# Rows of the experts added by TensorE as products with diagonal weight matrices in the closing stage of a hybrid-trunk kernel

## What is computed

```python
h_res = h_res + concat([y_conv, y_attn, y_hgrn]) @ w_out[l]
h_res = h_res + _hier_moe(_rmsnorm(h_res, ffn_norm[l]), ...)   # y = sum over 2 experts of weight * row
return _rmsnorm(h_res, final_norm)[:, N_META:]

def _rmsnorm(x, g):
    y = xf * lax.rsqrt(jnp.mean(xf * xf, axis=-1, keepdims=True) + EPS)
    return y * g
```

## Time and profile before

| | |
|---|---|
| time, median of 3 runs | 526.74 us (524.3 to 526.88) |
| time of the profiled execution | 522.46 us |
| its span, first to last instruction | 520.6 us |
| mean granted TensorE clock in it | 0.97 |
| PE busy | 482.1 us (93%) |
| DVE busy | 284.5 us (55%) |
| ACT busy | 154.7 us (30%) |
| DMA, mean over the span | 275 GB/s |

### The profile page before, as it was taken

The page is one execution under the profiler, slowest core; times in us unless marked ns, Lnnn a source line. Parts: engine busy times, 40 slices in busy tenths (PEclk is TensorE's granted clock), DMA queues, the critical chain, the costliest instruction groups (busy, mean ns, idle before and its releaser), DMA issues.

```text
span 520.6 us, 11031 instructions
## 1 busy us (share of the span) xinstructions
PE 482.1 (93%) x4503; PEld 323.9 (62%) x4503; DVE 284.5 (55%) x694; ACT 154.7 (30%) x386; POOL 48.6 (9%) x58
## 2 busy tenths in 40 slices
PE   5999999999998899999999999999999999895772
PEld 4888889888786455456556556575565555354430
DVE  3787998899668856337364433333343222231267
ACT  6420267410345334221134322222122111111143
POOL 3410000000001000000111011312102111000000
PEclk9999999999999999999989999999999999977887
DMA  8990000000009899419887999999999999999984
GB/s 277 356 374 36 0 2 0 1 1 1 3 7 358 287 421 412 186 42 364 278 299 299 353 403 346 409 414 418 416 415 412 418 415 416 416 417 416 413 330 162
DMA packets 38020, 143.03 MB, mean 275 GB/s; under 512 B 5166, under 2 KB 12519, under 8 KB 29393
## 3 DMA queue, kind: packets, MB, share of 16 engines
q1 hardware_dynamic: 31920, 131.03, 64.4%
q0 software_dynamic: 5760, 10.89, 5.9%
q10 hardware_dynamic: 288, 0.39, 0.2%
HBM read 133.73 MB, written 17.30 MB: 290 GB/s over the span
## 4 chain that ended last, share of the span: by engine, by line
PE 73%; DMA 11%; DVE 9%; SPq 3%; issue 2%; ACT 1%; POOL 1%; DVEq 0%; POOLq 0%
PE bank L1534 12%; PE bank L1872 11%; PE bank L1736 11%; PE bank L1880 6%; PE bank L1895 6%; DMA area_g<-in_w_exp_up 5%; PE bank L1544 4%; DMA area_g<-expert_out 4%; PE bank L1903 3%; PE bank L1474 3%; PE bank L1865 3%; PE bank L1678 2%; DVE area_m L932 2%; SPq L513 1%; DMA expert_out<-area_m,cst 1%
## 5 line engine op out<-in xcount | busy, mean ns | idle before, releaser
L1736 PE MATMUL bank<-area_w,area_m 128*128 128x512 f32 x128 | 56.7, 594 | 0.4 <-issue 0.4
L932 DVE SCALAR_TENSOR_TENSOR area_m<-area_g,cols,area_m 128x512 f32<-128x512 f32 x60 | 41.4, 745 | 0.0
L1872 PE MATMUL bank<-area_w,area_m 128*64 128x256 f32 x320 | 39.9, 394 | 1.2 <-ACT area_m L1984 1.2
L1736 PEld LDWEIGHTS bank<-area_w,area_m 128*128 128x128 f32 x128 | 23.6, 190 | 26.9 <-issue 26.9
L1872 PEld LDWEIGHTS bank<-area_w,area_m 128*64 128x64 f32 x320 | 22.7, 141 | 16.5 <-issue 5.1
L1872 PE MATMUL bank<-area_g,area_m 128*64 128x256 f32 x256 | 31.1, 384 | 0.7 <-DMA area_g<-in_w_exp_up 0.7
L2097 DVE COPY cst<-bank 128x128 f32<-128x128 f32 (+1 forms) x38 | 9.9, 261 | 32.1 <-PE bank L1886 23.4
L2106 DVE TENSOR_TENSOR cst<-cst,bank 64x128 f32<-64x128 f32 x20 | 5.9, 293 | 38.4 <-ACT cst L2022 33.3
L2115 DVE COPY area_m<-bank 64x512 f32<-64x512 f32 x20 | 13.9, 694 | 22.8 <-PE bank L1895 22.7
L1880 PE MATMUL bank<-area_w,area_m 128*32 128x128 f32 x576 | 22.4, 307 | 3.7 <-DMA area_w<-in_w_exp_up 3.7
L1872 PEld LDWEIGHTS bank<-area_g,area_m 128*64 128x64 f32 x256 | 17.3, 136 | 12.4 <-issue 3.9
(11 more groups left out here) (443 smaller groups left out, 898.0 us busy)
## 6 DMA issues: line engine op xcount, KB each, us to landing
area_w<-in_w_exp_gate SPq DMA_DIRECT2D x14, 1024.0 KB
area_w<-in_w_exp_up SPq DMA_DIRECT2D x14, 1024.0 KB
area_g<-in_w_exp_gate SPq DMA_DIRECT2D x14, 1024.0 KB, 17.2
area_g<-in_w_exp_up SPq DMA_DIRECT2D x14, 1024.0 KB, 18.2
area_g<-in_w_exp_down SPq DMA_DIRECT2D x14, 1024.0 KB
area_w<-in_w_exp_down SPq DMA_DIRECT2D x14, 1024.0 KB, 16.5
area_w<-in_w_in SPq DMA_DIRECT2D x7, 1024.0 KB, 14.4
area_w<-in_w_out SPq DMA_DIRECT2D x2, 2048.0 KB, 17.2
```

The costliest lines, as they stand in the source:

```text
L932: ins = V.scalar_tensor_tensor(out=mixT[:, i, :], in0=src, scalar=w, in1=mixT[:, i, :], op0=ALU.mult, op1=ALU.add)
L1736: ins = T.matmul(bank[7][:, :], mixT[:, k, j * P:(j + 1) * P], w_out_sb[:, n, k, :], start=(k == 0), stop=(k == KT - 1))
L1872: ins = T.matmul(out_b[h * BC:(h + 1) * BC, 0:2 * P], x[:, k, :], w_gate_up[slot][:, :, k, h * P:(h + 1) * P], start=(k == 0), stop=(k == ...
```

## The change

The banks of PSUM are declared in pairs, so that one instruction of DVE or ACT can read 1024 columns (two banks). Each tile's whole sum is to stand in one pair (`total[j]`). For tiles 1 to 3 PE adds everything: the residual as a product with the identity, the last column as before, and the two expert rows of each token as products with two diagonal 128 x 128 matrices that hold the tile's weights (`rows_weighted`). DVE makes these six matrices (`row_weights`) between `gated(40)` and `act_turned(40)`, in the space that slot 6's weights have left. ACT's statistics and DVE's norm then read the sums from the banks. Tile 0 is added by DVE as before. The residual product of tile 1 takes tile 2's place before block 41's gate and up products, and that of tile 2 goes between block 41's down product and the wait for its copied rows.

```diff
-        bank = [ctx.enter_context(nc.psum_tensor(f"bank{i}", [P, 512], F32)) for i in range(8)]
+        bank_pair = [ctx.enter_context(nc.psum_tensor(f"bank_pair{i}", [P, 1024], F32)) for i in range(4)]
+        bank = [bank_pair[i // 2][:, i % 2 * 512:(i % 2 + 1) * 512] for i in range(8)]
...
-        MIX_BANK = ((2, 3), (1, 4), (7, 0), (5, 6))
-        WHOLE = 2
+        SUM_PAIR = (2, 1, 0, 3)
+        total = [bank_pair[i][:, :] for i in SUM_PAIR]
+        weight_of = [area_x[:, 0:2 * ET * P].rearrange("p (j k n) -> p j k n", j=ET, k=2)[:, j] for j in range(ET)]
+        ROOM_FROM = max(LAST_OF[RING - 1::RING]) + 1
...
-            for j in range(NT):
-                act.wait_ge(summed, j + 1)
-                row_stats(j, 0)
+            act.wait_ge(summed, 1)
+            row_stats(0, 0, xr[0])
+            for j in range(1, NT):
+                act.wait_ge(mixed, j + 1)
+                row_stats(j, 0, total[j])
...
+            def row_weights():
+
+                dve.wait_ge(gu_done, ROOM_FROM)
+                for j in range(1, NT):
+                    for k in range(2):
+                        V.tensor_scalar(weight_of[j - 1][:, k, :], ident, w_rest[:, k, j:j + 1], None, ALU.mult).then_inc(diag_ready, 1)
...
                 y_out(b_ - 1)
                 gated(b_)
+                if b_ == NB - 2:
+                    row_weights()
...
-                dve.wait_ge(mixed, 2 * j + 2)
-                for n in range(2):
-                    h = slice(n * 512, (n + 1) * 512)
-                    ins = V.tensor_tensor(xr[j][:, h], bank[MIX_BANK[j][n]][:, :], xr[j][:, h], ALU.add)
-                ins.then_inc(summed, 1)
-
-            def token_sums(j):
-
-                dve.wait_ge(d_x[j], 16 + 32)
-                for n in range(2):
-                    dve.wait_ge(mixed, 2 * j + n + 1)
-                    h = slice(n * 512, (n + 1) * 512)
-                    V.scalar_tensor_tensor(out=xr[j][:, h], in0=ye[0][:, j, h], scalar=w_rest[:, 0, j:j + 1],
-                                           in1=bank[MIX_BANK[j][n]][:, :], op0=ALU.mult, op1=ALU.add).then_inc(first_sum, 1)
-                dve.wait_ge(first_sum, 2 * j + 2)
-                V.scalar_tensor_tensor(out=xr[j], in0=ye[1][:, j, :], scalar=w_rest[:, 1, j:j + 1], in1=xr[j],
-                                       op0=ALU.mult, op1=ALU.add).then_inc(summed, 1)
+                dve.wait_ge(mixed, j + 1)
+                V.tensor_tensor(xr[j], total[j], xr[j], ALU.add).then_inc(summed, 1)
...
-            for j in range(WHOLE):
-                rows_ahead(j)
-            for j in range(WHOLE):
-                last_added(j)
-            row_norm(0, 0)
-            for j in range(WHOLE, NT):
-                token_sums(j)
-                row_norm(j - 1, 0)
-            row_norm(NT - 1, 0)
+            rows_ahead(0)
+            last_added(0)
+            row_norm(0, 0, xr[0])
+            for j in range(1, NT):
+                row_norm(j, 0, total[j])
...
+            def rows_weighted(j, last):
+
+                pe.wait_ge(d_x[j], 16 + 32)
+                for k in range(2):
+                    for o, h in halves_of(j):
+                        ins = T.matmul(o, weight_of[j - 1][:, k, :], ye[k][:, j, h], start=False, stop=last and k == 1)
+                return ins
...
             def last_rows():
 
+                resid_in(2, True)
                 pe.wait_ge(y_lo, NB)
                 pe.wait_ge(y_hi, NB)
-                for j in range(NT):
-                    if j == ET:
-                        resid_in(j)
-                    for n in range(2):
-                        T.matmul(bank[MIX_BANK[j][n]][:, :], mix_flat[0:LAST_ROWS, j * P:(j + 1) * P],
-                                 yb[LAST % 2][0:LAST_ROWS, n * 512:(n + 1) * 512], start=j < WHOLE, stop=True).then_inc(mixed, 1)
+                last_column(0, True, True).then_inc(mixed, 1)
+                pe.wait_ge(diag_ready, 2 * ET)
+                for j in range(1, ET):
+                    rows_weighted(j, False)
+                    last_column(j, False, True).then_inc(mixed, 1)
+                last_column(ET, True, False)
+                resid_in(ET, False)
+                rows_weighted(ET, True).then_inc(mixed, 1)
...
                     pe.wait_ge(mix_ready, 3)
-                    for j in range(WHOLE, ET):
-                        resid_in(j)
+                    resid_in(1, True)
```

More of the change, by code:

```diff
@@ L2074, in experts_scalar @@
                     act.wait_ge(m_xT, m + 1)
-                    A_.activation(xT_half(0, 0), bank_half(0), ACT.Copy).then_inc(m_xTa, 1)
+                    A_.activation(xT_half(0, 0), bank_half(0), ACT.Copy).then_inc(m_xTr, 1)
                     act.wait_ge(m_gu, m + 1)
@@ L2192, in row_norm @@
                 for c in [slice(0, D)] if j < NT - 1 else [slice(0, D // 2), slice(D // 2, D)]:
-                    V.scalar_tensor_tensor(out=ye[0][:, j, c], in0=xr[j][:, c], scalar=rstd[:, j:j + 1], in1=gain_out[:, c],
+                    V.scalar_tensor_tensor(out=ye[0][:, j, c], in0=src[:, c], scalar=rstd[:, j:j + 1], in1=gain_out[:, c],
                                            op0=ALU.mult, op1=ALU.mult).then_inc(o_ready, 1)
-            for j in range(WHOLE):
-                rows_ahead(j)
-            for j in range(WHOLE):
-                last_added(j)
-            row_norm(0, 0)
-            for j in range(WHOLE, NT):
-                token_sums(j)
-                row_norm(j - 1, 0)
-            row_norm(NT - 1, 0)
+            rows_ahead(0)
[3 more added lines that the diff above has]
+                row_norm(j, 0, total[j])
             with dve.If(more > 0):
+                for j in range(1, NT):
+                    V.tensor_copy(xr[j], total[j]).then_inc(summed, 1)
                 with dve.Fori(0, more) as m:
                     dve.wait_ge(m_xT, m + 1)
-                    V.tensor_copy(xT_half(0, 1), bank_half(1)).then_inc(m_xTv, 1)
+                    V.tensor_copy(xT_half(0, 1), bank_half(1)).then_inc(m_xTr, 1)
                     dve.wait_ge(m_sg, m + 1)
@@ L2219, in experts_vector @@
                 for j in range(NT):
-                    row_norm(j, NT)
+                    row_norm(j, NT, xr[j])
         def experts_tensor(pe):
@@ L2289, in gain_spread, with halves_of, resid_in, last_column @@
                          start=True, stop=True).then_inc(mix_turned, 1)
-            def resid_in(j):
+            def halves_of(j):
+                return [(total[j][:, h], h) for h in (slice(0, 512), slice(512, D))]
+            def resid_in(j, first):
                 if j == ET:
                     pe.wait_ge(d_spill, 32)
-                for n in range(2):
-                    T.matmul(bank[MIX_BANK[j][n]][:, :], ident, xr[j][:, n * 512:(n + 1) * 512], start=True, stop=False)
+                for o, h in halves_of(j):
+                    T.matmul(o, ident, xr[j][:, h], start=first, stop=False)
+            def rows_weighted(j, last):
+                pe.wait_ge(d_x[j], 16 + 32)
+                for k in range(2):
+                    for o, h in halves_of(j):
+                        ins = T.matmul(o, weight_of[j - 1][:, k, :], ye[k][:, j, h], start=False, stop=last and k == 1)
+                return ins
+            def last_column(j, first, last):
+                for o, h in halves_of(j):
+                    ins = T.matmul(o, mix_flat[0:LAST_ROWS, j * P:(j + 1) * P], yb[LAST % 2][0:LAST_ROWS, h], start=first, stop=last)
+                return ins
             def last_rows():
+                resid_in(2, True)
                 pe.wait_ge(y_lo, NB)
                 pe.wait_ge(y_hi, NB)
-                for j in range(NT):
-                    if j == ET:
-                        resid_in(j)
-                    for n in range(2):
-                        T.matmul(bank[MIX_BANK[j][n]][:, :], mix_flat[0:LAST_ROWS, j * P:(j + 1) * P],
-                                 yb[LAST % 2][0:LAST_ROWS, n * 512:(n + 1) * 512], start=j < WHOLE, stop=True).then_inc(mixed, 1)
+                last_column(0, True, True).then_inc(mixed, 1)
[6 more added lines that the diff above has]
+                rows_weighted(ET, True).then_inc(mixed, 1)
             def x_of(k):
```

19 lines of the change are left out of this document (9 added, 10 removed).

## The result

The changed kernel took 529.66 us in the median of 20 runs (527.69 to 534.23), the kernel before 526.0 us (521.11 to 529.2, 20 runs on the same chips). The ratio is 1.0108, with a 95% interval of 1.0085 to 1.0132: 1.1% slower, some 5.7 us (4.5 to 6.9). The medians differ by less, 3.7 us: the runs of the kernel before fall into a group up to 524.4 us and one from 525.8 us on, and their median lies at the edge between the two, while the means differ by 5.4 us. One run of a later version (528.52 us, the work shared, run once more) was in the slower of the chip's two states and isn't in that version's ratio. The profiled execution of the changed kernel took 529.36 us, with a span of 527.5 us, 6.9 us more than that of the profile before.

The account below looks back on a forecast made before the run. DVE's 19 us of additions and norms were taken to set the end. PE's end at 520.49 plus 0.07, 1.75 and 3.96 gave a 526.27 us span, +5.7 on 526.74: 532.4 us, range 529.0 to 535.0.

Parts of the forecast that it names:

- The tail's share: From the last column's first product to the end of the span: forecast 501.41 to 526.27, against 20.55 us before.
- The head's: From block 40's first product to the last column's first: 1.36 us later, all from the six matrices.
- The price of a product and their count: From the last column on: PE has 22 products instead of 10, at 0.86 us each, with 0.16 us behind the last.
- Behind PE's end: Tile 3's statistics and norm: 0.07 us to ACT's start, 1.75 to the norm, 3.96 to the span's end; bank reading 0.
- The six matrices: On DVE between gated(40) and block 40's copy: six at 0.286 us, copy 1.36 us late, none of it regained.
- Tile 2's residual hidden at no cost, full clock behind it: Behind block 41's down product: two products, 1.72 us, fit the 1.76 us wait for ACT's copies; 0 at full clock.
- Rival 1: Half clock again for 3.4 us around 500 us, tile 2's residual no longer hidden: +7.4 us, 534.1 us; chance 0.19.
- Rival 2: Closing stage: tile 0's reloaded rows land later than profiled, moving the kernel before more: +3.7 us, 530.4 us; chance 0.13.
- Rival 3: Closing stage: a diagonal product costs PE under 0.60 us; at 0.43 us the change is -3.8 us, 522.9 us; chance 0.04.
- Rival 4: Change not felt: matrices hidden, rows late, clock full throughout; +2.3 us, 529.0 us, within no change; chance 0.09.

Follow-up runs that it names:

- the work shared, run once more: Repeat against the kernel before: DVE adds expert rows of tiles 1 and 2, PE all of tile 3, matrices behind gated(41); ratio 0.9933.
- tile 3 alone: Against the kernel before: only tile 3 added wholly by PE, its matrices behind gated(41), no residual products between blocks 40 and 41; ratio 0.999.
- The shared version: Against the kernel before: DVE adds expert rows of tiles 1 and 2, PE their residuals and all of tile 3; ratios 0.9972 and 0.9933.

## Why the prediction was right

The forecast was 526.74 us plus 5.7 us; the ratio gives 5.7 us. The mechanism is the forecast one: PE's products become the end of the kernel. The tail's share was forecast as 4.31 us (526.27 - 501.41 less 20.55) and came as 4.33. The head's was forecast as 1.36 us, and its parts came otherwise, one smaller and one that the sum didn't have; that the whole is met to a tenth of a us is luck, as the ratio is only known to 1.2 us either way. In absolute time the median of 529.66 us is 2.7 us under the forecast of 532.4 and only 0.7 us above the lower end of the range, since 526.74 was the median of three runs and the medians differ by less than the ratio says.

- **The price of a product and their count**: 22 x 0.86 + 0.16 = 19.08 us was forecast from the last column's first product to PE's end; it was 19.12 (502.62 to 521.74). Leaving out six took 5.18 us off the tail. This is the main term, and it is shown.
- **Behind PE's end**: 0.07, 1.75 and 3.96 us were forecast; 0.03 (521.74 to 521.77), 1.71 (to 523.48) and 4.0 (to 527.5) came. Reading the bank pair costs nothing:

```profile
L2192 DVE SCALAR_TENSOR_TENSOR area_w<-bank_pair,stat,gain_out 128x1024 f32<-128x1024 f32 x2 | 2.6, 1282 | 6.3 <-ACT stat L2069 6.3
...
L2192 DVE SCALAR_TENSOR_TENSOR area_w<-w_sums,stat,gain_out 128x1024 f32<-128x1024 f32 x1 | 1.3, 1285 | 1.8 <-ACT stat L2069 1.8
```

  These groups of the changed kernel have the norm at 1282 ns out of the banks and 1285 ns out of SBUF.
- **The six matrices**: 1.36 us of delay were forecast, 0.97 us came. The term was mis-sized: each is 280 ns long, which is what I had taken, but six in a row end after 1.26 us, since one starts 0.2 us behind the other. I had multiplied a duration where the distance of starts counts. That an fp32 `tensor_scalar` in SBUF runs at twice the one-element rate, as the Trainium skill (VectorE: DVE Perf Modes, the perf-mode tier table) states, can't be read from six instructions of one size.
- **Tile 2's residual hidden at no cost, full clock behind it**: right. The control without it cost 3.5 us in the tail.
- **What the sum didn't have**: half the clock between block 40 and block 41. Rival 1 had its mechanism, but behind 500 us; there the clock was full in every version with the gap filled, and the half clock was ahead of it instead. In the two profiles of the changed kernel it is worth 1.4 us (0.87 on the down product and 0.57 on the residual) and 1.7 us (3.67 less 1.98 on the residual). The +6.9 us between the two first spans are 0.97 + 1.44 + 4.33 and 0.1 us that came before. How much of the 1.4 us the average run has isn't shown: moving the matrices took 1.9 us off, give or take 2.2, and 0.97 of that would be the delay alone.
- **Rival 2** (rows late): PE never waited for a row in any profile. The 4.28 us between the profiled execution and the median, which the prediction could not place, are of the size of what the second profile of the kernel before had, 3.6 us, and there they came from the half clock in the mixer. Rows and PE moved together by 3.7 us, as the prediction's argument against this rival had it. **Rival 3** (a product under 0.60 us): it is 0.86. **Rival 4** (+2.3 us) is out by the interval, which begins at 4.5 us, and so is rival 1 as a whole (+7.4 us): the interval ends at 6.9.

What stays open is what puts the half clock into the head. In three profiles (changed, matrices behind gated(41), shared once more) it goes on from block 40 without a break. There the wait for the matrices can't be its cause: in the changed kernel the clock was at half ahead of the wait, and the other two have no such wait. Among the profiles whose clock was full at block 40's transpose, it fell in two of the three with that wait (not with one expert row left out), and in none of the five without it that have tile 1's residual products there. That leans to a second effect of the wait, and is no proof. Why the half clock sometimes outlasts block 40 no run here shows.

## What to carry to other kernels

Before work is handed to an idle engine, price it in that engine's own rows and compare with the slack that it has: here PE had 6 us and was given 12 products, 10.3 us, at 0.86 us for what costs DVE 0.65 to 0.7 us. Share such a stage until both engines end together, and put what one engine owes another (here the matrices) where the receiver is waiting for something else anyway. An idle stretch of PE isn't free to make. Filling one of 1.8 us won 3.5 us; taking two products (1.72 us) out of a stretch that ends with a transfer saved nothing and cost 1.5 to 3.2 us of clock behind it.

## What the runs showed that I had not expected

- DVE instructions that don't need each other's result overlap by some 0.08 us: six matrices of 280 ns end after 1.26 us, four after 0.88, two after 0.48, while a row addition that reads the sum of the one before it starts 0.03 us behind that one's end.
- The stretch between block 40 and block 41 can't be shortened by removing products: block 41's weights land 7.5 us behind block 40's (488.24 to 495.77 with the matrices behind gated(39), 489.96 to 497.51 with tile 3 alone), and in the kernel before PE took 7.8 us for it (486.17 to 493.96) and 7.55 in its second profile, so that 0.3 us is the most that fewer products could win.
- The shared version's two heads, 13.72 and 15.97 us, differ by 2.25 us with every wait of PE the same, only by where the half clock fell. The mixer, which no version touches, adds 0, 1.7 or 3.4 us in the same way. So a single profile of this kernel can't price an edit in the head to better than 2 us, nor any edit by the whole span to better than some 4 us; the tail, which kept to 0.3 us between profiles of one version, can be read from one.
